# Keys and values turned by VectorE in 32 by 32 blocks instead of by TensorE, with stores of 32 partitions

## What is computed

```python
h = rmsnorm(x, g_norm)
proj = h @ w_in                       # 1024 -> 10240 columns
u_p, z_p, q, k, v, z_r, gates = split(proj)
qh, kh = rope(q), rope(k) * 256 ** -0.5            # 4 heads of 256
vh = v                                             # 4 heads of 512
# chunkwise retention, for each head:
#   o = (q k^T * decay) v + (q * decay) s ;  s = g^C * s + (k * decay)^T v
# then norm of o, gates, pooling branch, output projection, residual, rmsnorm
```

## Time and profile before

| | us |
|---|---|
| runs | 2833.3, 2841.2, 3100.54 (median 2841.2) |
| the profiled execution's own time | 2833.37 |
| its span in the profile | 2831.6 |
| TensorE (PE) busy | 2782.2, 98% |
| VectorE (DVE) busy | 1808.3, 64% |
| ScalarE (ACT) busy | 1126.4, 40% |
| GpSimd (POOL) busy | 684.8, 24% |
| granted TensorE clock | 0.997 of full |

### The profile page before, as it was taken

How to read it: one execution, slowest core, us unless ns; L and a number is a source line. 1 busy time by engine, 2 the same in 40 slices (tenths; PEclk the granted TensorE clock), 3 DMA queues, 4 the chain that set the end, 5 groups by cost and what they waited for, 6 DMA issues and landing times.

```text
span 2831.6 us, 36714 instructions
## 1 busy us (share of the span) xinstructions
PE 2782.2 (98%) x13504; PEld 2249.1 (79%) x13504; DVE 1808.3 (64%) x2588; ACT 1126.4 (40%) x1901; POOL 684.8 (24%) x456
## 2 busy tenths in 40 slices
PE   6999999999999999999999999999999999999998
PEld 5888888888877777777777787877887888788876
DVE  8667566667555365655755566676677667766775
ACT  5444444444554444443434433333333333333332
POOL 5253433434332223425334330000000000000000
PEclk9999999999999999999999999999999999999999
DMA  4544444454564344453444458487648764876496
GB/s 144 197 146 155 173 147 158 156 179 145 180 223 153 113 156 162 147 186 125 163 154 154 165 200 307 141 278 289 246 145 283 289 239 150 283 290 234 153 340 261
DMA packets 281849, 552.80 MB, mean 195 GB/s; under 512 B 24216, under 2 KB 166872, under 8 KB 270527
## 3 DMA queue, kind: packets, MB, share of 16 engines
q1 hardware_dynamic: 266279, 541.73, 53.5%
q10 hardware_dynamic: 15168, 8.46, 1.0%
q0 software_dynamic: 224, 0.26, 0.0%
HBM read 375.59 MB, written 175.14 MB: 194 GB/s over the span
## 4 chain that ended last, share of the span: by engine, by line
PE 90%; DVE 4%; DMA 2%; issue 2%; ACT 1%; POOL 0%; ACTq 0%; SPq 0%; DVEq 0%; POOLq 0%
PE bank L1310 28%; PE bank L1312 28%; PE bank L1311 28%; PE bank L1360 2%; PE bank L1383 1%; PE bank L1502 1%; DMA raw<-in_w_branch_ret 1%; DVE w_lo L2173 1%; DVE xa_lo L2173 1%; DVE xs L2187 1%; PE bank L1632 1%; PE bank L1620 0%; PE bank L1610 0%; DMA x_d<-x_out 0%; DMA raw<-in_w_branch_pool 0%
## 5 line engine op out<-in xcount | busy, mean ns | idle before, releaser
L1310 PE MATMUL bank<-xa_hi,wa_hi 128*128 128x512 f32 x2240 | 888.8, 397 | 5.5 <-ACT part_s L1864 3.2
L1312 PE MATMUL bank<-xa_hi,wa_lo 128*128 128x512 f32 x2240 | 873.6, 390 | 0.0
L1311 PE MATMUL bank<-xa_lo,wa_hi 128*128 128x512 f32 x2240 | 873.5, 390 | 0.0
L1310 PEld LDWEIGHTS bank<-xa_hi,wa_hi 128*128 128x128 f32 x2240 | 420.6, 188 | 107.8 <-issue 21.5
L1312 PEld LDWEIGHTS bank<-xa_hi,wa_lo 128*128 128x128 f32 x2240 | 420.5, 188 | 90.0
L1311 PEld LDWEIGHTS bank<-xa_lo,wa_hi 128*128 128x128 f32 x2240 | 421.1, 188 | 82.8
L2173 DVE TENSOR_TENSOR wa_lo<-w_raw,wa_hi 128x512 fp32r<-128x512 f32 x320 | 312.7, 978 | 165.9 <-ACT wa_hi L1857 165.1
L2173 DVE TENSOR_TENSOR wa_lo<-w_sum,wa_hi 128x512 fp32r<-128x512 f32 x240 | 194.2, 809 | 241.3 <-ACT wa_hi L1857 241.3
L2173 DVE TENSOR_TENSOR w_lo<-raw,w_hi 128x512 fp32r<-128x512 f32 (+1 forms) x288 | 181.9, 659 | 189.3 <-ACT w_hi L1971 189.2
L1857 ACT ACTIVATE wa_hi<-w_raw 128x512 fp32r<-128x512 f32 x320 | 201.2, 629 | 242.6 <-PE bank L1312 238.3
L1971 ACT ACTIVATE w_hi<-raw 128x512 fp32r<-128x512 f32 (+1 forms) x288 | 166.4, 603 | 306.6 <-PE bank L1312 208.5
(11 more groups left out here) (253 smaller groups left out, 4311.8 us busy)
## 6 DMA issues: line engine op xcount, KB each, us to landing
w_raw<-in_w_in SPq DMA_DIRECT2D x80, 1024.0 KB, 5.3
v_d<-turned SPq DMA_DIRECT2D x64, 512.0 KB, 3.2
qk_s<-qk_d SPq DMA_DIRECT2D x32, 1024.0 KB, 7.4
v_s<-v_d SPq DMA_DIRECT2D x32, 1024.0 KB, 11.5
raw<-in_w_branch_ret SPq DMA_DIRECT2D x128, 256.0 KB, 4.2
tabs<-in_c_rope SPq DMA_DIRECT2D x16, 1024.0 KB, 6.9
qk_d<-high SPq DMA_DIRECT2D x32, 512.0 KB, 4.6
qk_d<-c_low SPq DMA_DIRECT2D x32, 512.0 KB, 5.4
```

The lines of the kernel that those rows point to most:

```text
L1310: pe.matmul(out, lh, rh, start=first, stop=False, skip_group_check=onto)
L1311: pe.matmul(out, lh, rl, start=False, stop=False, skip_group_check=onto)
L1312: return pe.matmul(out, ll, rh, start=False, stop=last, skip_group_check=onto)
```

## The change

The 96 groups of four TensorE transposes are gone. In their place VectorE transposes `c_out` in blocks of 32 by 32: two instructions of 128x512 for each half t of the tokens (`turn_blocks`, at steps 0 and 1 of the next job), 96 in all. Values are turned in place, keys into `tabs`, which is then free only when the keys' low parts are made. `turn_high` and `turn_low` read these blocks from SBUF where they read a PSUM bank.

A block transpose exchanges feature and token only inside groups of 32 partitions. What is left of the transpose is done by the stores: a turned store is four DMAs of 32 partitions each, one for each group, for keys in runs of 64 floats in DRAM (256 bytes), for values of 128 floats (512 bytes). Value jobs take their weight columns in groups of 32 (`weight_columns`). Queries and keys have their features in another order too, and so each rotated store is four DMAs of 32 partitions with rows of 2 KB. A key job has 32 store issues behind it where it had 8, a query job 16 for 4, a value job 16 for 4. A chunk's keys are loaded by four DMAs of 32 partitions, and the final state is stored by four for each head. For key jobs `rope_low` comes before `turn_low` at steps 2 and 4, and the eight rotated stores of a half are issued ahead of its second turned store.

In the second stage the state update and the output product take their moving values in eight runs of 64 floats.

```diff
-        turned = at("turned", [P, TURNED, 2, 2, DK], F32R)
+        turned = at("turned", [P, TURNED, 8, 2, 2, BT], F32R)
...
-        kt_d = scratch("kt_d", [NB, HEADS, NC, P, 2, 2, DK])
-        v_d = scratch("v_d", [NB, HEADS, NC, P, 2, 2, DV])
+        kt_d = scratch("kt_d", [NB, HEADS, BT, T // BT, 2, BA, 2 * BT])
+        v_d = scratch("v_d", [NB, HEADS, NT, P, 2, BA, 4 * BT])
...
                 engine.wait_ge(rope_done, 2 * before(i, "q", "k") + 2)
+                if kind(i) == "k":
+                    engine.wait_ge(turn_lo, 4 * before(i + 1, "k", "v"))
...
-            return {"q": 64, "k": 64, "v": 0}.get(kind(j), 32)
+            return {"q": 64 * BA, "k": 64 * BA, "v": 0}.get(kind(j), 32)
...
+        def weight_columns(j, rows, e):
+
+            w = w_raw[:, j % 2, rows, :]
+            if kind(j) == "v":
+                return w.rearrange("p k (a e s) -> p k a e s", a=BA, e=2)[:, :, :, e, :]
+            return w[:, :, e * P:(e + 1) * P]
...
+        def blocks(j, t, e):
+
+            if kind(j) == "v":
+                return c_out[:, j % 2, t, e, :]
+            return tabs[:, :, t * T:(t + 1) * T].rearrange("p c (b e s) -> p e c b s", b=8, e=2)[:, e]
...
+            def rotated(j, t):
+                what, i, _part = JOBS[j]
+                b = 2 * (j // NJ) + t
+                sp.wait_ge(qk_lo_done, 2 * before(j, "q", "k") + t + 1)
+                dst = qk_d[b, i, "qk".index(what)]
+                for low, src in enumerate((qk_high[t], c_low[:, j % 2, t])):
+                    for a in range(BA):
+                        rows = dst[a % 2 * 2 * BT:(a % 2 + 1) * 2 * BT, low, a // 2]
+                        sp.dma_start(rows.rearrange("(e s) t -> s e t", e=2),
+                                     src[a * BT:(a + 1) * BT].bitcast(F32)).then_inc(c_stored[j % 2], 16)
...
-                        dst = kt_d[b, i, c] if what == "k" else v_d[b, i, c][:, :, :, part * DK:(part + 1) * DK]
-                        sp.dma_start(dst, turned[:, n % TURNED].bitcast(F32)).then_inc(t_stored[n % TURNED], 16)
+                        if what == "k" and c:
+                            rotated(j, q // 2)
+                        for a in range(BA):
+                            src = turned[a * BT:(a + 1) * BT, n % TURNED].bitcast(F32)
+                            if what == "v":
+                                dst = v_d[b, i, 2 * c:2 * c + 2, :, part, a].rearrange("n (b r) x -> r (n b) x", b=BA)
+                                sp.dma_start(dst, src.rearrange("r b h e s -> r b (h e s)"))\
+                                    .then_inc(t_stored[n % TURNED], 16)
+                                continue
+                            dst = kt_d[b, i, :, 8 * c:8 * c + 8, :, a, :].rearrange("r b h x -> r (b h) x")
+                            sp.dma_start(dst, src.rearrange("r b h e s -> r (b h) (e s)")).then_inc(t_stored[n % TURNED], 16)
...
+            def keys_of_chunk(s, b, h, c):
+                src = kt_d[b, h, :, 8 * c:8 * c + 8].rearrange("r (i b) h a x -> b r i (h a x)", b=BA)
+                for i in range(BA):
+                    dst = kt_s[s][i * BT:(i + 1) * BT, c].bitcast(F32).rearrange("p i h d -> p i (h d)")
+                    sp.dma_start(dst, src[i]).then_inc(tv_arrived[s][c], 16)
+
+            def values_of_chunk(s, b, h, c):
+                sp.dma_start(v_s[s][:, c].bitcast(F32).rearrange("p i a h x -> p i (a h x)"),
+                             v_d[b, h][2 * c:2 * c + 2].rearrange("i p g a x -> p i (g a x)")).then_inc(tv_arrived[s][c], 16)
...
+                    final = io["ret_prompt"][0, 0, p].rearrange("(e k a s) v -> a e s k v", e=2, k=2, a=2)
+                    for part in range(BA):
+                        sp.dma_start(final[part // 2, part % 2], state[part * BT:(part + 1) * BT, p]).then_inc(state_stored, 16)
...
-            def turn(j, q):
...
-                        mm = pe.transpose(banks[6 + q % 2][:, (2 * i + e) * P:(2 * i + e + 1) * P],
-                                          c_out[:, j % 2, t, e, tile * P:(tile + 1) * P], ident[:])
-                mm.then_inc(turn_mm, 1)
...
-                    if j and kind(j - 1) in ("k", "v") and 1 <= i < 5:
-                        turn(j - 1, i - 1)
...
-                act.wait_ge(turn_mm, n + 1)
-                act.activation(turned[:, n % TURNED, 0].rearrange("p i d -> p (i d)"), banks[6 + q % 2][:], ACT.Copy,
-                               scale=turn_scale(j)).then_inc(turn_hi, 1)
+                act.wait_ge(blocks_turned, n - q + 2 * (q // 2) + 2)
+                act.activation(turned_part(j, n, 0), turned_source(j, q), ACT.Copy, scale=turn_scale(j)).then_inc(turn_hi, 1)
...
+            def turn_blocks(j, t):
+                if kind(j) == "k":
+                    dve.wait_ge(rope_done, 2 * before(j, "q", "k") + t + 1)
+                elif t == 0:
+                    dve.wait_ge(c11_done, j + 1)
+                    dve.wait_ge(c12_done, j + 1)
+                else:
+                    dve.wait_ge(c21_done, j + 1)
+                    dve.wait_ge(c22_done, j + 1)
+                for e in range(2):
+                    src = c_out[:, j % 2, t, e, :]
+                    if kind(j) == "k":
+                        src = src.rearrange("p (c b s) -> p c b s", c=2, s=BT)
+                    dve.transpose(blocks(j, t, e), src).then_inc(blocks_turned, 1)
...
+                    if j and kind(j - 1) == "k" and i in (2, 4):
+                        rope_low(j - 1, i // 2 - 1)
...
+                    if j and kind(j - 1) in ("k", "v") and i == 0:
+                        turn_blocks(j - 1, 0)
                     if j and kind(j - 1) in ("q", "k") and i < 2:
                         rope(j - 1, 1, (i,))
+                    if j and kind(j - 1) in ("k", "v") and i == 1:
+                        turn_blocks(j - 1, 1)
...
-                    for t in range(2):
-                        if j and (kind(j - 1), i) in (("q", 2 + 2 * t), ("k", 3 + 2 * t)):
-                            rope_low(j - 1, t)
+                    if j and kind(j - 1) == "q" and i in (2, 4):
+                        rope_low(j - 1, i // 2 - 1)
```

More of the change, by code:

```diff
@@ L47 @@
 TURNED = 3
+BT = 32
+BA = P // BT
 X_SUM = {S1T1: 0, S2T2: 1, S3T3: 2, S4B22: 3}
@@ L659, in c_free, with like_weights, turned_part, turned_source @@
             if before(j - 1, "k", "v"):
-                engine.wait_ge(turn_mm, 4 * before(j - 1, "k", "v"))
+                engine.wait_ge(turn_lo, 4 * before(j - 1, "k", "v"))
+        def weight_columns(j, rows, e):
[3 more added lines that the diff above has]
+            return w[:, :, e * P:(e + 1) * P]
+        def like_weights(j, w):
+            return w.rearrange("p k (a s) -> p k a s", a=BA) if kind(j) == "v" else w
+        def blocks(j, t, e):
+            if kind(j) == "v":
+                return c_out[:, j % 2, t, e, :]
+            return tabs[:, :, t * T:(t + 1) * T].rearrange("p c (b e s) -> p e c b s", b=8, e=2)[:, e]
+        def turned_part(j, n, low):
+            return turned[:, n % TURNED, :, low]
+        def turned_source(j, q):
+            t, c = q // 2, q % 2
+            if kind(j) == "v":
+                return c_out[:, j % 2, t, :, c * CHUNK:(c + 1) * CHUNK].rearrange("p e (b s) -> p b e s", s=BT)
+            return tabs[:, c, t * T:(t + 1) * T].rearrange("p (b e s) -> p b e s", b=8, e=2)
         def turn_scale(j):
@@ L675, in all_turned_stored @@
             for i in range(TURNED):
-                engine.wait_ge(t_stored[i], 16 * len(range(i, n, TURNED)))
+                engine.wait_ge(t_stored[i], 16 * BA * len(range(i, n, TURNED)))
         def win_steps(sb, g, t):
@@ L770, in store @@
                     out = c_out[:, j % 2, t]
[L771 to L775, removed]
+                    if what == "q":
+                        rotated(j, t)
                     elif what == "z":
@@ L836, in _ @@
             for i in range(2):
-                sp.dma_start(qk_s[0][:, i].bitcast(F32), qk_d[0, 0, i]).then_inc(qk_arrived[0], 16)
+                head_piece(0, 0, i)
             all_turned_stored(sp, NJ)
@@ L1197, in weight_sums @@
             def weight_sums(j, steps):
-                b11, b12 = w_raw[:, j % 2, 0:KH, 0:P], w_raw[:, j % 2, 0:KH, P:2 * P]
-                b21, b22 = w_raw[:, j % 2, KH:KT, 0:P], w_raw[:, j % 2, KH:KT, P:2 * P]
+                b11, b12 = (weight_columns(j, slice(0, KH), e) for e in range(2))
+                b21, b22 = (weight_columns(j, slice(KH, KT), e) for e in range(2))
+                sums = [like_weights(j, w_sum[:, k]) for k in range(2)]
                 if 0 in steps:
```

98 lines of the change are left out of this document (39 added, 59 removed).

## The result

The changed kernel took 2847.18 us (median of 15 runs, 2842.61 to 2853.34), the kernel before 2835.47 (15 runs, 2833.3 to 2841.74 but for one of 3100.54, a slow execution that the ratio leaves out). The ratio is 1.004, with a 95% interval of 1.0032 to 1.0048. So the change costs 0.4%, where 2832 us and a gain of 1.4 us were forecast. The time is inside the range, and the sign is wrong.

The account below looks back on a forecast made before the run. PE, busy 98% of the span, was taken to bound the kernel. From 2833.4 us, 45.6 saved on turns, 39 lost to late stores and 5 in the second stage gave 2832 us; range 2796 to 2905.

Parts of the forecast that it names:

- Removed: the turns: First stage, PE: four transposes gone, 1.9 us for each of 24 jobs, 45.6 us saved, all on the path.
- Added on VectorE: First stage: 96 block transposes of 0.60 us; PE waits 1.2 us before product 6 behind each of eight key jobs.
- rival of a slow transpose: VectorE's block transposes take 1.2 us each, 2.4 us more in each key case: 2851 us; 5%.
- Added on the SP queue and in DMA: First stage: 32 store issues behind a key job land late; PE waits 4.8 us for each of eight, 39 us.
- Rival 3: Key stores' 256-byte packets take 60 ns, PE waits 146 us in all: 2939 us; over 2% slower from 44 ns; 18%.
- Rival 2: Stores of 32 partitions move at half rate, 0.60 us for 128 KB; the second stage pays 10 us: 2859 us; 27%.
- Second stage: Key loads become four DMAs each, 96 more issues of 0.43 us: at most 13 us, taken as 5 us lost.

Follow-up runs that it names:

- e4: The kernel before with its rotated stores each split into four DMAs of 32 neighbouring partitions: 2837.53 us, ratio 1.0006.
- e3: The kernel before with each chunk's key load split into four DMAs of all 128 partitions and a quarter of the columns: 2838.17 us, ratio 1.0011.
- e2: The kernel before with each chunk's key load split into four DMAs of 32 neighbouring partitions: 2862.12 us, ratio 1.0091.
- e1: The changed kernel with another DRAM layout of kt_d, each chunk's keys loaded by one DMA of 128 partitions: 2825.66 us, 0.9964 of the kernel before.
- e7: e1 with the rotated stores of half 1 issued ahead of the third turned store: 2823.86 us, 0.9958 of the kernel before.
- e8: e1 with key jobs' rotated stores as one DMA of 128 partitions each, result not the layer's: 2810.44 us, 0.9908 of the kernel before.

## Why the prediction was wrong, by its own steps

- **"Removed: the turns", 45.6 us: right.** Jobs behind value jobs went from 20.93 to 19.04 us (job 2 to job 3, after: 84.44 to 103.48), 1.9 as taken. In the second half of the jobs it was 22.21 to 20.31, the same 1.90.
- **"Added on VectorE": right.** 0.61 us a transpose (0.60 taken), wait before product 6 of 1.4 us (1.2). The rival of a slow transpose is refuted. One reading was off by a little: VectorE's stretch from 106.20 did have a gap, 0.97 us for ScalarE's `turned`.
- **"Added on the SP queue and in DMA", 39 us: mechanism and size right for one key job, too large in sum.** The first key job costs 4.8 us, as forecast; the next three 3.4, 3.9 and 3.6, the last four 2.6, 3.2, 3.0 and 3.1. These are 27.6 us; the whole stage gave 16.1 of 45.6, so 29.5 were lost in it. I had taken one schedule, that of job 3, for all eight. The last rotated store lands 34.1 us from the job's start for the first key job, but 32.8 to 33.3 for the next three. In the second half a job without turns is 20.3 us, in both kernels, so the store has 1.3 us more in which to land. There PE hardly waits for the landing any more; what is left is VectorE's addition before product 6, once in each of the two jobs behind a key job. Of the other 1.9 us, 1.4 are lost where the two halves of the tokens meet (jobs 38 to 40), which was priced at nothing.
- **Rival 3 and its rule: refuted.** 256-byte packets go at 21 ns, on the line of the prediction (10 ns and 38 ns for each KB), not 60. Its far end was a misreading, too: the 72 ns of rows 11 divide the time that SP was held by the packets, while the trace before lists packets of 4 bytes there at 9 ns on average. The read-modify-write below 512 bytes of the Trainium skill (DMA: Bandwidth & Descriptors, section Specifications) has no price that can be seen here: the queue took those stores at 0.55 to 0.65 us each.
- **Rival 2: the right rule, priced at the wrong place.** I weighed the port rule for the *stores* of 32 partitions. For stores e4 gives 0.51 us, packets a quarter longer and no loss of time that can be told; the loads are where it costs. The prediction did give it a second-stage cost, 10 us, with 27%.
- **"Second stage", 5 us: the step that failed.** It measured 27.5. The prediction priced the split key loads by their issues alone: 96 more of 0.43 us, "all of it on the path would be 13 us; I take 5". That part was even high: e3 shows that four wide loads cost 3.4 us. What was left out is that each of these DMAs goes to 32 neighbouring partitions. Such a load holds the DMA engines while they move less (343 in e2 in place of 385 GB/s before in the same 32 us; the earlier trace rows had 381 in 40 us), and what stands in the queue behind it is late: `v_s` lands in 13.1 us, not 11.5, the weights make ScalarE wait 12.2, not 7.9, and PE runs dry. Put in alone (e2) it costs 27.3 us; taken out (e1) it gives 21.5 back. I had the row that says where DMA is the limit, and I had the rule in rival 2, but did not put the one to the other.

The two errors had opposite signs: 9.5 us too much in the first stage and 22.5 too little in the second, 13 in all. This is the distance from the sum's -1.6 (-45.6 + 39 + 5) to +11.4. That the time came within 15 us of the forecast owes as much to this as to the working.

What stays open: in e1's trace some 4 us are still lost at the change of stages and 5.7 behind the last block's retention. The latter isn't steady (3.6 in e7, 2.0 in e8), and e1's profiled execution was 4.5 us over its median. The final state's narrow stores, the key load's runs of 1 KB and the strided weights are all possible causes; none was run alone.

## What to carry to other kernels

When a DMA is cut into pieces, price the place in SBUF that each piece touches, not only its issues and its packets: cut by columns or by every fourth partition, the key load was free to within 3.4 us; cut by neighbouring partitions it cost 25 to 27. Ask it first in stretches where the DMA share is near 1.00: there the cost is in GB/s, and falls on whoever queues behind. The narrow stores of e4, at a DMA share of 0.90, had slower packets and cost nothing that can be told. Compare stretches that do the same work, not the same microseconds, when one kernel runs ahead of the other. If a store must be narrow for the sake of its layout, choose the layout in DRAM so that the load that reads it can be wide, as e1 does; and a period worked out for the first of several jobs isn't that of the later ones until a row of theirs has been read.

## What the runs showed of the hardware that was not expected

- A load to 64 neighbouring partitions is as narrow as one to 32 (24.7 and 27.3 us for the same bytes, 268 and 272 ns for a packet of 4 KB in place of 159); one to every fourth partition isn't narrow at all (0.8 us, 161 ns).
- Stores from 32 neighbouring partitions, 128 KB each, went at 0.51 us, 256 GB/s, without a loss of time that can be told, though their 4 KB packets took some 200 ns in place of 160.
- Writes to DRAM in runs of 256 bytes cost 21 ns a packet on average.
- A block transpose of 128x512 floats takes 0.61 us from start to start, the same as an addition of that size (0.60).
- After 5.9 us without work PE's granted clock was 0.50 for the stretch that followed, and its matmuls started 0.43 us apart in place of 0.23. That is a second cost of this wait:

```profile
1730.61 0.79 PE L1370 MATMUL bank<-og_hi,w_hi 128*128 128x512 f32 x1 [5.88 <-DVE y L2522]
...
1731.62 0.63 PE L1372 MATMUL bank<-og_hi,w_lo 128*128 128x512 f32 x1
1732.05 0.63 PE L1370 MATMUL bank<-og_hi,w_hi 128*128 128x512 f32 x1
```
